# The sums of squares behind the norms: four fp32 matmuls with a column of ones, or four transposes and one VectorE sum over PSUM

## The chip, the cores and the metric

The kernel runs on one core of a Trainium2 chip. The time is device microseconds (us) of one execution. Three runs of the kernel before took 1218.58, 1219.01 and 1220.04 us.

## The reference, cut to what matters

A bidirectional encoder trunk of two layers over a sequence of 512 positions with 1024 features, all in float32. Each layer has two norms over all 1024 features (`g_mix` ahead of the attention part, `g_mlp` ahead of the MLP), two over 256 features (`g_q`, `g_kv`) and one per differential head over 128 features (`g_sub`, four heads); a last norm follows layer two.

```python
def _rmsnorm(x, g, eps=EPS):
    y = x * lax.rsqrt(jnp.mean(x * x, axis=-1, keepdims=True) + eps)
    return y * g

h = x
for l in range(DEPTH):
    z = _rmsnorm(h, g_mix[l]) @ w_in[l]
    c_q, c_kv = _rmsnorm(z[:, 0:256], g_q[l]), _rmsnorm(z[:, 256:512], g_kv[l])
    # eight latent heads from c_q, c_kv; four differential heads from z:
    o = _diff_attention(dq, dk, dv, lam, slopes)        # two softmax maps a head, their difference on dv
    o = _rmsnorm(o, g_sub[l], SUBLN_EPS) * (1.0 - lam_init)
    h = h + concatenate([o_mla, o], axis=-1) @ w_out[l]
    h = h + square(relu(_rmsnorm(h, g_mlp[l]) @ w_up[l])) @ w_down[l]
return _rmsnorm(h, g_final)
```

## The kernel before

Activations lie transposed: features on the 128 partitions, the 512 positions along a row. Every large product is three matmuls on two-part operands (a high and a low part), made by `three` (L1494). Each engine has one program in one fixed order, written out by hand, and engines wait for one another on counting semaphores. Weight blocks come by DMA into two staging buffers; ScalarE makes the high part (L738), VectorE or GpSimd the low part (L1050, L631).

A norm's statistic is needed once per position, summed over features, which is over partitions. It is made in these steps, always in one PSUM bank, `MISC_BANK` (bank 5):

1. ScalarE squares and VectorE adds up the squares of all feature tiles into `ss` (128 x 512); for a differential head, ScalarE leaves the squares of the one tile in `tmp_s[:, 1, :]` (L811).
2. TensorE, `stat_c` (L1504): for each of four groups of 128 positions, one fp32 matmul with the squares as the stationary operand and a column of ones as the moving one. It leaves positions on partitions, in columns 0 to 3 of the bank. It raises `misc_done`.
3. VectorE, `stat_col` (L1062): waits for `misc_done`, writes `rc` = sum/count + eps (128 x 4, L1065), raises `misc_free`.
4. GpSimd, `power` (L608): waits for that, writes `rs` = rc to the power -0.5 (L611), raises `pow_done`.
5. TensorE, `stat_b` (L1513): waits for `pow_done`, then four transposes (L1519) of the broadcast `rs` put the scale of each position on all partitions. VectorE reads it: `stat_row` (L1068) copies it to `rb` or `rb_c`; for a differential head L1354 multiplies with it.

`stat_c` and `stat_col` run 15 times: once for `mix_c` (only in the second layer; the first layer's statistic of the input is made in another way), and in both layers for `q_c`, `kv_c`, four times `sub{g}_c`, and `mlp_c`. The last norm does not use them.

What stands around them. In the part of the latent norms TensorE runs `stat_c` for `q_c` behind the first of four blocks of the `dv` product and `stat_b` for it behind the second (L1742 to L1746); `kv_c` likewise behind the third and fourth. VectorE reaches `stat_col` of `q_c` behind the steps of the rotary key (`krf`, L1254 to L1263) and two `split`s (L1050). For `mlp_c` TensorE runs `stat_c`, half of an up projection's sum (12 matmuls), then `stat_b`. In attention, a loop over steps n: VectorE's order in a step is the inverse softmax sum (L1087), two fused score reads (L1080), then `stat_col` of a head (at n = 8, 12, 16, 20, ahead of L1092), the combination of the two maps (L1092) and the low part of the transposed map (L1112). The first sixteen steps are the differential heads', the next 32 the latent heads' (row maxima L1099, inverse sums L1106).

Of the kernel before, what the change touches and what calls it, by code (L numbers as in the profile page):

```python
# [6 lines left out]
F32 = mybir.dt.float32  # L7
F32R = mybir.dt.float32r
ALU = mybir.AluOpType
ACT = mybir.ActivationFunctionType  # L10
AX_X = mybir.AxisListType.X

P = 128
SEQ, D_MODEL, DEPTH = 512, 1024, 2
KD = D_MODEL // P
TT = SEQ // P
# [197 lines left out]
def trunk(nc, x, w_in, g_mix, g_q, g_kv, w_uq, w_ukv, lam_q1, lam_k1, lam_q2, lam_k2,  # L214
# [3 lines left out]
    def place(name, shape, dt, at=None):  # L218
        size = 4 * int(math.prod(shape[1:]))
        if at is None:  # L220
            at = at_byte[0]
            at_byte[0] += -(-size // 32) * 32
        return nc.alloc_sbuf_tensor_at(name, shape, dt, offset=at)
# [37 lines left out]
    ss = place("ss", [P, SEQ], F32, scratch)  # L261
# [18 lines left out]
    ident = place("ident", [P, P], F32)  # L280
    ones = place("ones", [P, P], F32)
    mhalf = place("mhalf", [P, TT], F32)
    rc = place("rc", [P, TT], F32)
    rs = place("rs", [P, TT], F32)
    rs_mix = place("rs_mix", [P, TT], F32)
    g_rows = place("g_rows", [P, P], F32, region + 16 * kb)
    g_cols = place("g_cols", [P, G_ROWS], F32)
# [14 lines left out]
    with ExitStack() as ctx:  # L302
        bank = [ctx.enter_context(nc.psum_tensor(f"bank{b}", [P, SEQ], F32)) for b in range(8)]
        MISC_BANK, SC_BANKS, TR_BANKS, DV_BANKS = bank[5], bank[2:5], bank[6:8], [bank[2], bank[3], bank[6], bank[7]]
# [5 lines left out]
        def counter(name, per):  # L310

            sem = ctx.enter_context(nc.semaphore(name))
            per_layer[id(sem)] = per
            counters.append(sem)
            return sem

        def once(name):
            return ctx.enter_context(nc.semaphore(name))
# [8 lines left out]
        misc_done, misc_free = counter("misc_done", len(MISC)), counter("misc_free", len(MISC))  # L327
# [30 lines left out]
        u2_added = counter("u2_added", 3)  # L358
        h_turned, h_rows, rows_done, rows_added = (once(n) for n in ("h_turned", "h_rows", "rows_done", "rows_added"))
        sq_summed, mean_made, rs_made, g_out_in = (once(n) for n in ("sq_summed", "mean_made", "rs_made", "g_out_in"))  # L360
        left_made, x_squared, x_left = once("left_made"), once("x_squared"), once("x_left")
        chain_done = counter("chain_done", CHAIN)

# [7 lines left out]
        def val(sem, l, k):  # L371

            return (l + 1) * per_layer[id(sem)] + k
# [87 lines left out]
        def u_low(k):  # L461
            return u_lo[:, (k + KD // 2) % KD, :]
# [566 lines left out]

        @block.vector  # L1030
        def _(dve):
            chain = [0]

            def link(l, ins):

# [18 lines left out]
            def add_square(l, n, first):  # L1054
# [3 lines left out]
                else:  # L1058
                    dve.wait_ge(ss_acc, val(ss_acc, l, n))
                    nc.vector.tensor_tensor(ss[:, :], ss[:, :], tmp_s[:, n % 2, :], ALU.add).then_inc(ss_acc, 1)  # L1060

            def stat_col(l, m, count, eps):  # L1062

                dve.wait_ge(misc_done, val(misc_done, l, m + 1))
                nc.vector.tensor_scalar(rc[:, :], MISC_BANK[:, 0:TT], 1.0 / count, eps, ALU.mult, ALU.add  # L1065
                                        ).then_inc(misc_free, 1)

            def stat_row(l, m, dst):  # L1068
# [162 lines left out]
            for l in layers(dve):  # L1231
                chain[0] = 0

                if l:
                    stat_col(l, MISC_AT["mix_c"], D_MODEL, EPS)
                else:
                    split(0, RING + 1)
# [29 lines left out]
                for b in range(TT):  # L1267
                    split(l, BLOCK_AT[("dv", b)] + RING)
                    if b == 0:
                        stat_col(l, MISC_AT["q_c"], LORA, EPS)  # L1270

                        add_square(l, KD + 2, True)
                        add_square(l, KD + 3, False)
                    if b == 1:
                        stat_row(l, MISC_AT["q_b"], rb_c[:, :])
                        for t in range(KC):
                            nc.vector.scalar_tensor_tensor(out=e_t[:, t, :], in0=e_t[:, t, :],
                                                           scalar=cols(g_cols, G_Q + t, l, KC), in1=rb_c[:, :],
                                                           op0=ALU.mult, op1=ALU.mult).then_inc(c_ready, 1)
                    if b == 2:  # L1280
                        stat_col(l, MISC_AT["kv_c"], LORA, EPS)
                        for t in range(KC):
                            dve.wait_ge(c_hi_made, val(c_hi_made, l, t + 1))
                            nc.vector.tensor_tensor(c_lo[:, t, :], e_t[:, t, :], c_hi[:, t, :].bitcast(F32), ALU.subtract
                                                    ).then_inc(c_lo_made, 1)
# [27 lines left out]
                for n in range(STEPS + 5):  # L1313
# [15 lines left out]
                    g, r = divmod(n - 8, TT)  # L1329
# [159 lines left out]
        def _(pe):  # L1489
            def three(acc, terms, first, last):  # L1490

                for t, ((a_hi, a_lo), (b_hi, b_lo)) in enumerate(terms):
                    for m, (a, b) in enumerate(((a_hi, b_hi), (a_hi, b_lo), (a_lo, b_hi))):
                        mm = nc.tensor.matmul(acc, a, b, start=first and t == 0 and m == 0,  # L1494
                                              stop=last and t == len(terms) - 1 and m == 2)
                return mm

            def wtile(s, k, w=P):
                return w_hi[:, s, k * w:(k + 1) * w], w_lo[:, s, k * w:(k + 1) * w]

            def u(k):
                return u_hi[:, k, :], u_low(k)

            def stat_c(l, m, src=None):  # L1504

                pe.wait_ge(misc_free, val(misc_free, l, m))
                for tt in range(TT):
                    mm = nc.tensor.matmul(MISC_BANK[:, tt:tt + 1], (ss[:, tt * P:(tt + 1) * P] if src is None  # L1508
                                                                   else src[:, tt * P:(tt + 1) * P]),
                                          ones[:, 0:1], start=True, stop=True)  # L1510
                mm.then_inc(misc_done, 1)

            def stat_b(l, m, k):  # L1513
# [173 lines left out]
            for k in range(KD):  # L1687
                pe.wait_ge(u_lo_made, val(u_lo_made, 0, k + 1))
                mm = nc.tensor.matmul(bank[BANK["cq0"]][:, :], wtile(SLOT[0], k)[0], u_low(k), start=False, stop=k == KD - 1)
# [9 lines left out]
            for l in layers(pe):  # L1699


                if l:
                    for use in ("cq0", "cq1"):
                        pe.wait_ge(w_hi_made, val(w_hi_made, l, BLOCK_AT[(use, 0)] + 1))
                        pe.wait_ge(*low_ready(l, BLOCK_AT[(use, 0)]))
                        pe.wait_ge(*taken(l, use))
                    for t in range(KD):
                        pe.wait_ge(u_lo_made, val(u_lo_made, l, t + 1))
                        for use in ("cq0", "cq1"):
                            mm = three(bank[BANK[use]][:, :], [(wtile(SLOT[BLOCK_AT[(use, 0)]], t), u(t))], t == 0, t == KD - 1)  # L1710
                            if t == KD - 1:
                                mm.then_inc(proj_done, 1)
                    pe.wait_ge(ss_acc, val(ss_acc, l, KD))
                    stat_c(l, MISC_AT["mix_c"])
                    head_sum(l, "ckv0", range(KD))
                    stat_b(l, MISC_AT["mix_b"], 0)
                    head_sum(l, "ckv1", range(KD))
# [4 lines left out]
                for t in range(KD):  # L1722
                    for m in range(2):
                        mm = nc.tensor.matmul(bank[BANK["kr"]][:, :], w_hi[:, SLOT[BLOCK_AT[("kr", 0)]], t * P:(t + 1) * P],  # L1724
                                              u(t)[m], start=(t == 0 and m == 0), stop=(t == KD - 1 and m == 1))
# [5 lines left out]
                for b in range(TT):  # L1731
# [3 lines left out]
                    for tt in range(TT):  # L1735
                        for k in range(2):
                            kk = 2 * b + k
                            mm = three(DV_BANKS[tt][:, :], [((u(kk)[0][:, tt * P:(tt + 1) * P],
                                                              u(kk)[1][:, tt * P:(tt + 1) * P]),
                                                             wtile(s, k, SEQ))], kk == 0, kk == KD - 1)  # L1740
# [23 lines left out]
                for n in range(STEPS + 1):  # L1764
                    if DSTEPS < n + 2 < STEPS:
                        scores(l, n + 2)
                    g, r = divmod(n - TT - 2, TT)
# [217 lines left out]
```

## Time and profile before

| | |
|---|---|
| median of three runs | 1219.01 us |
| the profiled execution, its own time | 1218.42 us |
| its span in the trace | 1216.1 us |
| TensorE (PE) busy | 1191.5 us, 98% |
| VectorE (DVE) busy | 892.4 us, 73% |
| ScalarE (ACT) busy | 601.8 us, 49% |
| GpSimd (POOL) busy | 541.8 us, 45% |
| share of the chain that ended last | PE 92%, DVE 4%, ACT 2% |

An engine is called busy while an instruction of its own is in flight; matmuls overlap, so a busy TensorE need not be at its peak. The chain that ended last is followed back from the last instruction, at each step to what released it. In the rows further down a time is us from the span's start; "PEld" is the load of a stationary operand. Two instructions of one engine overlap a little in such rows: the next starts about 0.08 us before the one ahead of it is written as ended, unless it waits.

### The profile page before, as it was taken

The numbers are of one execution on the slowest core, as the hardware profiler recorded it, in microseconds if no ns is written. First come the engines' busy times: TensorE is split into PE (matmuls) and PEld (weight loads), VectorE is DVE, ScalarE is ACT, GpSimd is POOL, SyncE is SP. The second block draws the span as 40 slices with busy tenths as digits, with TensorE's granted clock in tenths as the row PEclk, the third lists the DMA queues.
The fourth block names the chain that finished last, engine by engine and source line by source line (L and its number), as shares of the span: only waits on it lengthen the run. The fifth ranks groups of instructions, "written<-read, shape, count | busy, mean of one in ns | idle before, by whom it ended". The sixth has DMA issues, their size and how long they took to land.

```text
span 1216.1 us, 16360 instructions
## 1 busy us (share of the span) xinstructions
PE 1191.5 (98%) x5700; PEld 975.7 (80%) x5700; DVE 892.4 (73%) x1341; ACT 601.8 (49%) x986; POOL 541.8 (45%) x339
## 2 busy tenths in 40 slices
PE   8999889999999999999999999999999999999997
PEld 7877578888888888888888766788888888888886
DVE  4658967756778776879846688677658678767896
ACT  6345666744544344435423466676444444344443
POOL 1001344622865576556510023446047664766462
PEclk9999999999999999999999998999999999999999
DMA  6521101124234322430324211102252234223402
GB/s 192 138 55 61 45 18 35 53 87 153 75 86 137 115 87 85 130 111 30 104 66 112 61 37 43 36 18 85 73 172 87 78 113 139 86 72 120 139 7 98
DMA packets 128131, 104.55 MB, mean 86 GB/s; under 512 B 5514, under 2 KB 107956, under 8 KB 128052
## 3 DMA queue, kind: packets, MB, share of 16 engines
q1 hardware_dynamic: 127840, 103.50, 28.4%
q8 instruction: 47, 0.77, 0.3%
q14 instruction: 32, 0.26, 0.1%
q10 hardware_dynamic: 84, 0.02, 0.0%
q0 software_dynamic: 128, 0.00, 0.0%
HBM read 99.84 MB, written 2.10 MB: 84 GB/s over the span
## 4 chain that ended last, share of the span: by engine, by line
PE 92%; DVE 4%; ACT 2%; issue 1%; DMA 1%; POOL 0%; SPq 0%; POOLq 0%; DVEq 0%; ACTq 0%
PE bank L1494 82%; PE bank L1561 3%; PE bank L1589 3%; PE bank L1533 2%; DVE pt_lo L1112 1%; PE bank L1508 1%; PE bank L1724 1%; DVE e_t L1092 1%; DMA xin<-in_x 1%; ACT pt_hi L770 0%; DVE k_pack L1158 0%; PE bank L1519 0%; PE bank L1669 0%; DVE v_pack L1151 0%; DVE e_t L1080 0%
## 5 line engine op out<-in xcount | busy, mean ns | idle before, releaser
L1494 PE MATMUL bank<-u_hi,w_hi 128*128 128x512 f32 x760 | 299.4, 394 | 0.3
L1494 PE MATMUL bank<-u_hi,w_lo 128*128 128x512 f32 x760 | 296.1, 390 | 0.0
L1494 PE MATMUL bank<-u_lo,w_hi 128*128 128x512 f32 x760 | 295.8, 389 | 0.0
L738 ACT ACTIVATE w_hi<-stage 128x1024 fp32r<-128x1024 f32 (+3 forms) x141 | 136.4, 976 | 221.0 <-DMA stage<-in_w_up 91.3
L1050 DVE TENSOR_TENSOR w_lo<-stage,w_hi 128x1024 fp32r<-128x1024 f32 (+2 forms) x116 | 134.8, 1171 | 59.8 <-ACT w_hi L738 59.3
L1494 PEld LDWEIGHTS bank<-u_hi,w_hi 128*128 128x128 f32 x760 | 142.7, 188 | 30.8 <-issue 2.5
L1494 PEld LDWEIGHTS bank<-u_hi,w_lo 128*128 128x128 f32 x760 | 142.6, 188 | 30.2
L1494 PEld LDWEIGHTS bank<-u_lo,w_hi 128*128 128x128 f32 x760 | 142.8, 188 | 28.6
L738 ACT ACTIVATE w_hi<-b 128x1024 fp32r<-128x1024 f32 x84 | 88.9, 1059 | 131.8 <-PE bank L1494 105.2
L1494 PE MATMUL bank<-w_hi,quad_hi 128*128 128x512 f32 x392 | 152.6, 389 | 0.0
L1494 PE MATMUL bank<-w_hi,quad_lo 128*128 128x512 f32 x392 | 152.5, 389 | 0.0
L1494 PE MATMUL bank<-w_lo,quad_hi 128*128 128x512 f32 x392 | 152.5, 389 | 0.0
L1050 DVE TENSOR_TENSOR w_lo<-b,w_hi 128x1024 fp32r<-128x1024 f32 x84 | 121.6, 1448 | 24.3 <-ACT w_hi L738 24.3
L1439 DVE TENSOR_TENSOR acc<-acc,bank 128x512 f32<-128x512 f32 x216 | 136.5, 674 | 0.0
L1112 DVE TENSOR_TENSOR pt_lo<-bank,pt_hi 128x512 fp32r<-128x512 f32 x96 | 65.9, 686 | 44.8 <-ACT pt_hi L770 44.2
L1453 DVE SCALAR_TENSOR_TENSOR tmp_y<-bank,rb 128x512 f32<-128x512 f32 x64 | 43.7, 688 | 69.4 <-PE bank L1494 68.7
L611 POOL TENSOR_TENSOR rs<-rc,mhalf 128x4 f32<-128x4 f32 x14 | 18.8, 1340 | 154.4 <-DVE rc L1065 154.4
L1494 PEld LDWEIGHTS bank<-w_lo,quad_hi 128*128 128x128 f32 x392 | 73.6, 188 | 15.3
L1494 PEld LDWEIGHTS bank<-w_hi,quad_lo 128*128 128x128 f32 x392 | 73.6, 188 | 15.2
L1494 PEld LDWEIGHTS bank<-w_hi,quad_hi 128*128 128x128 f32 x392 | 73.6, 188 | 15.2
L636 POOL TENSOR_TENSOR b<-b,b 128x1024 f32<-128x1024 f32 x28 | 81.4, 2909 | 1.1
L624 POOL TENSOR_SCALAR e_t<-e_t,coefs 128x512 f32<-128x512 f32 x64 | 44.3, 694 | 80.5 <-DVE coefs L1106 79.7
(233 smaller groups left out, 2263.4 us busy)
## 6 DMA issues: line engine op xcount, KB each, us to landing
stage<-in_w_up SPq DMA_DIRECT2D x64, 512.0 KB, 4.0
b<-in_w_down SPq DMA_DIRECT2D x56, 512.0 KB, 3.4
stage<-in_w_in SPq DMA_DIRECT2D x32, 512.0 KB, 3.9
stage<-in_w_out SPq DMA_DIRECT2D x16, 512.0 KB, 3.6
stage<-in_w_down SPq DMA_DIRECT2D x8, 512.0 KB, 3.4
xin<-in_x SPq DMA_DIRECT2D x4, 512.0 KB, 6.7
stage<-in_w_ukv SPq DMA_DIRECT2D x4, 512.0 KB, 3.3
out<-yout SPq DMA_DIRECT2D x8, 256.0 KB, 2.3
```

The source lines that it names most:

```text
L611: nc.gpsimd.tensor_tensor(dst[:, :], rc[:, :], mhalf[:, :], ALU.pow).then_inc(pow_done, 1)
L624: nc.gpsimd.tensor_scalar(e_t[:, t, :], e_t[:, t, :], coefs[:, t:t + 1], 1.0, ALU.mult, ALU.mult).then_inc(p_ready, 1)
L636: nc.gpsimd.tensor_tensor(dst[:, :], a[:, :], b[:, :], ALU.subtract).then_inc(t_made, 1)
L738: last = nc.scalar.activation(hi(w_hi, s)[:, :, d:d + n], st(r)[:, :, f:f + n], ACT.Copy)
L1050: last = nc.vector.tensor_tensor(dst, st(r)[:, :, f:f + n], hi(w_hi, s)[:, :, d:d + n].bitcast(F32), ALU.subtract)
L1112: nc.vector.tensor_tensor(piece(pt_lo), TR_BANKS[n % 2].rearrange("p (k c) -> p k c", k=TT), piece(pt_hi).bitcast(F32), ALU.subtract).then ...
L1439: last = nc.vector.tensor_tensor(dst, dst, src, ALU.add)
L1453: nc.vector.scalar_tensor_tensor(out=tmp_y[:, i % 2, :], in0=bank[BANK[use]][:, :], scalar=0.0, in1=rb[:, :], op0=ALU.max, op1=ALU.mult).t ...
L1494: mm = nc.tensor.matmul(acc, a, b, start=first and t == 0 and m == 0, stop=last and t == len(terms) - 1 and m == 2)
L1533: mm = nc.tensor.matmul(SC_BANKS[(2 * n + m) % 3][:, :], a[rows, hd, q], b[rows, :], start=p == 0, stop=p == 2)
L1561: mm = nc.tensor.transpose(TR_BANKS[n % 2][:, kt * P:(kt + 1) * P], e_slot(t)[:, kt * P:(kt + 1) * P], ident[:, :])
L1589: mm = nc.tensor.matmul(MISC_BANK[:, q], v_pack[:, kt, hd, :, :].rearrange("p a c -> p (a c)"), pt[:, kt, q], start=(kt == 0 and pt is pt_ ...
```

## The change

`stat_c` transposes the four 128 x 128 groups of squares into the bank, 512 columns in all, in place of the four matmuls with the column of ones. On VectorE a new `row_sums` waits for `misc_done`, sums the bank over its last 128 columns in each of four groups (one `tensor_reduce`, 128 x 4 from 128 x 512, into the new tile `rsums`) and waits for its own semaphore; `stat_col` then works on `rsums` in SBUF. `misc_free` is still raised by the instruction that writes `rc`. Nothing else is altered: no order of work, no buffer but the new 16 bytes a partition.

```diff
+    rsums = place("rsums", [P, TT], F32)
+        cols_summed = once("cols_summed")
-            chain = [0]
+            chain, summed = [0], [0]
+            def row_sums(l, m):
+
+                dve.wait_ge(misc_done, val(misc_done, l, m + 1))
+                summed[0] += 1
+                nc.vector.tensor_reduce(rsums[:, :], MISC_BANK.rearrange("p (t c) -> p t c", t=TT), AX_X, ALU.add
+                                        ).then_inc(cols_summed, 1)
+                dve.wait_ge(cols_summed, summed[0])
+
             def stat_col(l, m, count, eps):
 
-                dve.wait_ge(misc_done, val(misc_done, l, m + 1))
-                nc.vector.tensor_scalar(rc[:, :], MISC_BANK[:, 0:TT], 1.0 / count, eps, ALU.mult, ALU.add
+                row_sums(l, m)
+                nc.vector.tensor_scalar(rc[:, :], rsums[:, :], 1.0 / count, eps, ALU.mult, ALU.add
                                         ).then_inc(misc_free, 1)
                 # stat_c:
                 pe.wait_ge(misc_free, val(misc_free, l, m))
                 for tt in range(TT):
-                    mm = nc.tensor.matmul(MISC_BANK[:, tt:tt + 1], (ss[:, tt * P:(tt + 1) * P] if src is None
-                                                                   else src[:, tt * P:(tt + 1) * P]),
-                                          ones[:, 0:1], start=True, stop=True)
+                    r = slice(tt * P, (tt + 1) * P)
+                    mm = nc.tensor.transpose(MISC_BANK[:, r], ss[:, r] if src is None else src[:, r], ident[:, :])
                 mm.then_inc(misc_done, 1)
```

## Rows read from the trace of the kernel before

**Rows 1.** The page: busy time of each engine, share of the span, instructions.

```profile
PE 1191.5 (98%) x5700; PEld 975.7 (80%) x5700; DVE 892.4 (73%) x1341; ACT 601.8 (49%) x986; POOL 541.8 (45%) x339
```

**Rows 2.** Windows by engine: stretch, busy us (instructions), granted clock, DMA share, GB/s.

```profile
140.00:160.00 20.00, 15.63 (x83) 11.23 (x82) 17.00 (x38) 12.58 (x29) 6.11 (x7) 1.00 0.07 14
...
740.00:760.00 20.00, 18.48 (x84) 13.67 (x85) 17.25 (x37) 12.29 (x28) 6.08 (x8) 0.84 0.07 14
```

**Rows 3.** The chain that ended last, 115 to 182 us: start, us, what.

```profile
121.62 0.80 PE bank L1508 x8
...
122.44 0.04 DVE rc L1065
```

**Rows 4.** Timeline of PE, first layer: start, us, engine, line, operation, xcount.

```profile
42.87 0.95 PE L1508 MATMUL bank<-ones,ss 128*128 128x1 f32 x8
43.67 0.49 PE L1494 MATMUL bank<-w_hi,u_hi 128*128 128x512 f32 x1
...
49.26 0.60 PE L1519 MATMUL bank<-ident,rs 128*128 128x128 f32 x4
49.61 0.48 PE L1494 MATMUL bank<-w_hi,u_hi 128*128 128x512 f32 x1
...
61.56 0.60 PE L1519 MATMUL bank<-ident,rs 128*128 128x128 f32 x4
```

**Rows 5.** Timeline of DVE outside attention; in brackets the idle time before.

```profile
42.07 0.68 DVE L1256 TENSOR_TENSOR krf<-bank,krf 64x512 f32<-64x512 f32 x1 [3.12 <-ACT krf L882]
42.79 0.68 DVE L1259 TENSOR_TENSOR krf<-krf,ck 64x512 f32<-64x512 f32 x1
...
47.66 0.15 DVE L1065 TENSOR_SCALAR rc<-bank 128x4 f32<-128x4 f32 x1
...
292.78 0.16 DVE L1065 TENSOR_SCALAR rc<-bank 128x4 f32<-128x4 f32 x1 [6.17 <-PE bank L1508]
```

**Rows 6.** Timeline of POOL: the powers of q_c, kv_c, mlp_c, and q_c in layer two.

```profile
47.90 1.13 POOL L611 TENSOR_TENSOR rs<-rc,mhalf 128x4 f32<-128x4 f32 x1 [23.73 <-DVE rc L1065]
57.89 1.39 POOL L611 TENSOR_TENSOR rs<-rc,mhalf 128x4 f32<-128x4 f32 x1 [8.86 <-DVE rc L1065]
...
293.02 1.93 POOL L611 TENSOR_TENSOR rs<-rc,mhalf 128x4 f32<-128x4 f32 x1 [38.22 <-DVE rc L1065]
...
647.20 1.12 POOL L611 TENSOR_TENSOR rs<-rc,mhalf 128x4 f32<-128x4 f32 x1 [24.28 <-DVE rc L1065]
```

**Rows 7.** Timeline of PEld: stationary loads of stat_b for q_c, mlp_c, q_c again.

```profile
49.08 0.53 PEld L1519 LDWEIGHTS bank<-ident,rs 128*128 128x128 f32 x4
...
295.25 0.58 PEld L1519 LDWEIGHTS bank<-ident,rs 128*128 128x128 f32 x4
...
648.43 0.58 PEld L1519 LDWEIGHTS bank<-ident,rs 128*128 128x128 f32 x4
```

**Rows 8.** Timeline of DVE in the first layer's attention, 117 to 181 us.

```profile
121.68 0.68 DVE L1080 CUSTOM_DVE_ANT_0 e_x<-bank,consts 128x512 f32<-128x512 f32 x1
...
122.44 0.16 DVE L1065 TENSOR_SCALAR rc<-bank 128x4 f32<-128x4 f32 x1
...
139.25 0.16 DVE L1065 TENSOR_SCALAR rc<-bank 128x4 f32<-128x4 f32 x1 [0.28 <-PE bank L1508]
...
141.17 0.69 DVE L1342 TENSOR_TENSOR k_pack<-krf,k_pack 64x512 fp32r<-64x512 f32 x1 [0.49 <-ACT k_pack L922]
...
158.34 0.68 DVE L1099 TENSOR_REDUCE nmx<-bank 128x1 f32<-128x512 f32 x1
158.94 0.15 DVE L1065 TENSOR_SCALAR rc<-bank 128x4 f32<-128x4 f32 x1
...
159.86 0.16 DVE L1106 RECIPROCAL coefs<-rsum 128x1 f32<-128x1 f32 x1 [0.18 <-ACT e_t L759]
...
173.15 0.16 DVE L1065 TENSOR_SCALAR rc<-bank 128x4 f32<-128x4 f32 x1 [1.66 <-PE bank L1508]
...
175.37 0.69 DVE L1112 TENSOR_TENSOR pt_lo<-bank,pt_hi 128x512 fp32r<-128x512 f32 x1 [0.21 <-ACT pt_hi L770]
```

## The prediction

> **What bounds the kernel now.** I read the page first, for the busy shares: TensorE is busy 98% of the span, VectorE 73% [rows 1]. So in most places only a shorter or a later TensorE moves the end. Next the windows, for the places where that does not hold: in the differential heads' stretch TensorE is busy 15.63 us of 20 while VectorE has 17.00 [rows 2]. The reader is to see two regimes there: TensorE dense outside, VectorE nearly dense and TensorE with holes inside, from about 121 to 178 us and again in layer two. The chain of waits agrees: it runs on TensorE up to the first head's `stat_c` (121.62, 0.80 us) and goes over to VectorE's `rc` [rows 3]. Last, the timelines of each engine around the 15 statistics, for what is late next.
>
> Seven of the 15 (`mix_c` once, `q_c`, `kv_c`, `mlp_c` twice each) lie where TensorE is dense; eight (`sub0_c` to `sub3_c`, twice) where VectorE's order sets the pace.
>
> **Part 1, TensorE's own time.** From the first record of `stat_c` to the matmul behind it takes 43.67 - 42.87 = 0.80 us. Four transposes of 128x128 fp32 are already in the trace, those of `stat_b`: 49.61 - 49.26 = 0.35 us [rows 4]. So each replacement saves 0.45 us of TensorE where TensorE is dense. The last record ends 0.95 us behind the first before and 0.60 behind with transposes, so VectorE can be released 0.35 us earlier. The bounds of the saving are 0.80 - 0.60 = 0.20 (if the new transposes don't overlap what follows) and 0.45. I take 0.45, since the four in the row run between the same matmuls.
>
> **Part 2, the sum on VectorE.** The trace has a TENSOR_REDUCE of 128x512 from PSUM, of 0.68 us, with 0.60 us to the next instruction when nothing waits (158.34 to 158.94) [rows 8]. It writes one value per partition and not four; that costs at most a few cycles, I add nothing. But the new sum is waited for by the instruction behind it. The same thing is in the trace once, a 0.68 us instruction that the next one waits for: 42.07 to 42.79, 0.72 us [rows 5]. So one sum delays VectorE by 0.60 to 0.72 us; I take 0.72. The instruction for `rc` stays what it is.
>
> A rule of the Trainium skill speaks to this. The row shows 0.72 us with the wait against 0.60 without [rows 5, 8]. "VectorE: DVE Perf Modes", section "The DRAIN you can't avoid", has it that a semaphore between chained VectorE instructions costs nothing extra; by it the sum would be 0.60 us. The same page's "Rules for kernel authors" calls `tensor_reduce` the slowest VectorE operation and advises against it on a hot path, which is a rule against this change.
>
> **Part 3, where TensorE is dense.** Here the question is whether the power on GpSimd still comes before `stat_b`, for TensorE stops there if not.
>
> `q_c`, first layer. VectorE comes to `stat_col` late: it has been busy from 42.07 on and writes `rc` at 47.66, long after TensorE's sum was done at 43.82, so the earlier release is worth nothing. The power runs 47.90 to 49.03 [rows 6], and TensorE loads the first operand of `stat_b` at 49.08 [rows 7]: the power is only just in time. With the sum in front the power ends at 49.75, and the load comes at about 49.80. TensorE is there 0.45 us earlier than before, at 48.63, and stands still for 1.17 us. Net +0.72 us. Behind it on TensorE stands the third `dv` block and everything else. Second layer: power ends at 648.32, load at 648.43, slack 0.11; measured from a time line that `mix_c` has moved up, net 0.72 - 0.06 = +0.66 (0.05 is the gap between a power's end and the load in layer one).
>
> `kv_c`. The power ends at 59.28 and `stat_b` starts at 61.56 [rows 4, 6]; slack 2.28 against 0.72 + 0.45. The saving is kept: -0.45 each. `mix_c` has 24 matmuls between `stat_c` and `stat_b` as `q_c` has, but VectorE there waits for TensorE, as at `mlp_c`; -0.45.
>
> `mlp_c`. VectorE waits 6.17 us for TensorE and starts at once [rows 5], so it gains the 0.35 us. The power starts at 293.02 + 0.72 - 0.35 = 293.39 and ends at 295.32; the load goes from 295.25 to 295.37. Net +0.1 instead of -0.45. I take the second layer alike.
>
> Sum: 0.72 + 0.66 - 3 x 0.45 + 2 x 0.1 = +0.25 us (bounds: -3.15 if the powers are in time by a margin that the GpSimd rows don't show, which are rough; +1.0 if the saving is only 0.20).
>
> **Part 4, the differential heads.** What the idle times behind each `rc` absorb, first layer [rows 8]:
> - `sub0_c` (122.44): VectorE is free at 122.36, so 0.08 us of the earlier release can be used. Net 0.72 - 0.07 = +0.65, on the chain [rows 3]. Behind it wait L1092 and L1112, for them TensorE's transposes, for these ScalarE. Bounds 0.37 and 0.72.
> - `sub1_c` (139.25): VectorE idled 0.28 before, and idles 0.49 before L1342 behind it. 0.72 - 0.28 = 0.44 is less than 0.49: 0.
> - `sub2_c` (158.94): no idle time before; 0.18 before 159.86, of which about 0.27 can be filled with the overlap of two instructions. Net +0.45, bounds 0.3 and 0.72.
> - `sub3_c` (173.15): 1.66 idle before, so the full 0.35 is gained, then 0.21 before 175.37 and about 0.06 of overlap. Net +0.1.
>
> That is 1.2 us a layer, 2.4 us in both, with bounds 1.2 and 3.4. TensorE's 0.45 us is worth nothing here except as the release used above.
>
> **The sum.** +0.25 + 2.4 = +2.65 us on the profiled execution: 1218.42 + 2.65 = 1221.1. That execution lies 0.59 us under the median of the runs shown, so against those 1219.01 + 2.65 = 1221.7 us, +0.22%. What a measurement of this kernel can tell from no change is about 0.2%, 2.4 us.
>
> **The rivals.**
>
> *Hidden on VectorE, TensorE's saving remains (faster).* The place is `stat_b` of `q_c` and `mlp_c` and the differential stretch. If in that stretch idle time further on absorbs the sums, and the power is in time at the four places of part 3, all seven savings count: 7 x 0.45 = 3.15 us, 1215.9 us. It decides from a slack of 1.17 us between power and load. For it: VectorE is idle 27% of the span. Against it: the slacks read are 0.05, 0.11 and 0.30 us, and `rc` of the first head is on the chain.
>
> *A wait on one's own semaphore costs nothing.* Each sum is then 0.60 us. Eight of the 15 pay in full (`q_c`, `mlp_c`, `sub0_c`, `sub2_c`, twice each): 8 x 0.12 = 0.96 us less, 1220.7 us, within 0.2%. For it: nothing in these rows; against it, 42.07 to 42.79. The page named in part 2 would have it so.
>
> *The longer stretch costs TensorE's clock.* In layer two the granted clock fell to 0.84 over 740 to 760 us, in layer one it stayed at 1.00 with TensorE less busy [rows 2]. A mean of 0.84 is 1.2 in place of 2.4 GHz for 0.32 of the 20 us, 6.4 us, in which 3.2 us of full-speed work is not done; the same stretch of layer one has holes of 4.37 us. So one fall costs between 0 and 3.2 us; I take 1.25, nearer to hidden. One more fall per layer gives 1221.7 + 2.5 = 1224.2 us. What speaks for it is the fall that is there; against it, that the longer holes grow by 1.2 us in 40 only.
>
> *Only half arrives in the differential stretch.* ScalarE's and GpSimd's order there are chains of their own; if they are late already, `sub2_c` and half of `sub0_c` go under: 2.4 - 1.5 = 0.9, and 1220.2 us.
>
> **How the numbers follow.** The forecast 0.45, whose own range is 1220.7 to 1223.0. The free wait 0.1, half arriving 0.22, clock 0.13, hidden 0.1. Slower by over 0.2% is above 1221.45: 0.4 of the forecast and of its near neighbours on the upper side, with the clock, makes 0.53. Faster is nearly all of the hidden case: 0.08. Within: 0.39. Range 1218.3 to 1224.2: it leaves out most of the hidden case and the ends of the clock's.
>
> **What would show each step.** Between `stat_c`'s first record and the next matmul 0.35 us in dense places (part 1). A TENSOR_REDUCE of 0.68 us and 0.72 us to `rc` (part 2). TensorE standing about 1.2 us before `stat_b` of `q_c`, with GpSimd's L611 as releaser, and 0.5 us before that of `mlp_c` (part 3). The stretch from `sub0_c` to the dense part longer by 1.2 us in each layer (part 4). The forecast is wrong if those stops are missing, if the heads' stretch keeps its length, or if the clock falls elsewhere than before.

## The result: 0.24% slower, and the profile after

The kernel with the change takes 1222.86 us (median of 14 runs, 1219.64 to 1224.93); the kernel before, run beside it, 1219.46 us (14 runs, 1218.32 to 1221.80). The ratio is 1.0024, with a 95% interval from 1.0015 to 1.0032: slower by 1.8 to 3.9 us, with 2.9 us in the middle (the two medians by themselves are 3.4 us apart). 1221.7 us had been forecast, 2.65 us above before. Two executions of kernels further down, one of 2401 us (TensorE's half alone) and one of 3099 us (the norms alone), count as slow and are left out of their medians and ratios.

The page of the changed kernel, busy time (us) by engine and then the chain that ended last by engine:

```profile
PE 1186.2 (97%) x5640; PEld 969.0 (79%) x5640; DVE 902.8 (74%) x1356; ACT 602.4 (49%) x986; POOL 540.9 (44%) x339
...
PE 84%; issue 7%; DVE 5%; ACT 1%; DMA 1%; POOL 1%; SPq 0%; POOLq 0%; ACTq 0%; DVEq 0%
```

TensorE has 60 matmul records fewer (15 statistics, 8 records each before, 4 now) and is busy 5.3 us less; VectorE has 15 instructions more and is busy 10.4 us more [rows 1]. 15 x 0.45 = 6.75 us and 15 x 0.69 = 10.3 us are what the parts would give. Neither sum is the change of the time: it depends on where they lie.

The statistics themselves. Timeline of PE after, first layer (start, us, engine, line, operation; in brackets the idle time before and who ended it):

```profile
57.83 0.60 PE L1519 MATMUL bank<-ident,ss 128*128 128x128 f32 x4
58.19 0.48 PE L1504 MATMUL bank<-w_hi,u_hi 128*128 128x512 f32 x1
...
123.69 0.60 PE L1519 MATMUL bank<-ident,tmp_s 128*128 128x128 f32 x4
...
181.06 0.94 PE L1504 MATMUL bank<-k_pack,q_pack 128*128 128x512 f32 x3 [0.77 <-DVE k_pack L1168]
```

From `stat_c` (of `kv_c` here) to the matmul behind it takes 58.19 - 57.83 = 0.36 us, where it took 0.80 at `q_c` before [rows 4]. Timeline of DVE after, the sum of `q_c` and that of `sub0_c`:

```profile
44.15 0.68 DVE L1266 TENSOR_TENSOR krf<-bank,krf 64x512 f32<-64x512 f32 x1 [2.58 <-ACT krf L884]
...
49.74 0.68 DVE L1068 TENSOR_REDUCE rsums<-bank 128x4 f32<-128x512 f32 x1
50.46 0.17 DVE L1075 TENSOR_SCALAR rc<-rsums 128x4 f32<-128x4 f32 x1
...
124.53 0.69 DVE L1068 TENSOR_REDUCE rsums<-bank 128x4 f32<-128x512 f32 x1
125.25 0.17 DVE L1075 TENSOR_SCALAR rc<-rsums 128x4 f32<-128x4 f32 x1
125.33 0.75 DVE L1102 SCALAR_TENSOR_TENSOR e_t<-e_t,coefs 128x512 f32<-128x512 f32 x1
```

The sum stands 0.72 us ahead of `rc` at both places, and at `sub0_c` what is behind it (L1102) starts 0.80 us after the sum. Where the chain that ended last ran on TensorE and then over one `rc` [rows 3], it now crosses all four sums of the first layer's heads:

```profile
124.61 0.61 DVE rsums L1068
...
141.81 0.61 DVE rsums L1068
...
161.84 0.61 DVE rsums L1068
...
176.17 0.70 DVE rsums L1068
```

That a sum lies on this chain doesn't say that it costs its 0.7 us: the one at 141.81 (`sub1_c`) took the place of idle time, and its stage kept its length (below).

Windows of the granted clock, after (columns as in rows 2), and one of the kernel before behind it:

```profile
5.00:10.00 5.00, 2.93 (x18) 2.46 (x17) 2.81 (x4) 2.63 (x4) 0.00 (x0) 0.83 1.11 345
10.00:15.00 5.00, 5.00 (x18) 4.00 (x17) 2.21 (x4) 3.22 (x6) 1.04 (x1) 0.50 0.87 222
...
140.00:160.00 20.00, 16.09 (x90) 11.17 (x88) 17.07 (x40) 14.47 (x32) 5.86 (x7) 1.00 0.07 15
740.00:760.00 20.00, 17.15 (x89) 12.02 (x86) 17.00 (x39) 14.39 (x32) 5.82 (x7) 0.91 0.07 14
```

```profile
10.00:15.00 5.00, 5.00 (x31) 4.28 (x30) 3.91 (x8) 3.65 (x7) 1.04 (x1) 1.00 0.87 220
```

This is a trap in the pair. From 10 to 15 us TensorE was granted 0.50 in the execution after (1.2 GHz all through) and 1.00 before (2.4 GHz), although nothing that runs there was altered. By the first `stat_b` the two time lines are 31.03 - 27.71 = 3.32 us apart, before the first changed instruction:

```profile
31.03 0.60 PE L1528 MATMUL bank<-ident,rs_mix 128*128 128x128 f32 x4
```

```profile
27.71 0.60 PE L1519 MATMUL bank<-ident,rs_mix 128*128 128x128 f32 x4
```

About 0.3 us of that is the second piece of the input, whose transposes start at 8.54 in place of 8.23 us; the rest goes with the clock. The spans differ by 1219.8 - 1216.1 = 3.7 us, so nearly all of this pair's difference is the start's. Read from it: the lengths of stages, from one named instruction to another. Not from it: the total; that comes from the runs. In us, from `stat_c` to `stat_c` unless said otherwise:

| stage | before | after | forecast | found |
|---|---|---|---|---|
| `q_c` to its `stat_b`, layer 1 | 6.39 | 5.92 | +0.72 | -0.47 |
| its `stat_b` to `kv_c` | 5.91 | 5.90 | 0 | 0 |
| `kv_c` to `sub0_c` | 66.28 | 65.86 | -0.45 | -0.42 |
| `sub0_c` to the first `k_pack` product | 56.17 | 57.37 | +1.2 | +1.20 |
| from there to `mlp_c` | 114.18 | 114.19 | 0 | 0 |
| `mlp_c` to `mix_c` | 328.88 | 328.87 | +0.1 | 0 |
| `mix_c` to `q_c`, layer 2 | 21.58 | 21.27 | -0.45 | -0.31 |
| `q_c` to its `stat_b` | 6.39 | 6.77 | +0.66 | +0.38 |
| its `stat_b` to `sub0_c` | 71.90 | 71.46 | -0.45 | -0.44 |
| `sub0_c` to the first `k_pack` product | 56.73 | 57.47 | +1.2 | +0.74 |
| from there to `mlp_c` | 114.19 | 114.17 | 0 | 0 |
| `mlp_c` to the end of the span | 324.63 | 324.54 | +0.1 | -0.1 |

The last column sums to +0.6 us; the 0.74 is against a stretch that the kernel before ran at 0.84 of the clock between 740 and 760 us [rows 2]. Against 56.17, its length at full clock, layer two's heads pay 1.30 and the sum is about +1.1 (after, these 20 us ran at 0.91).

The stops of TensorE at `stat_b`, from the weight loads (PEld) after, at `q_c`, `mlp_c` and `q_c` of layer two, with the powers of the last two on POOL behind them:

```profile
51.88 0.41 PEld L1528 LDWEIGHTS bank<-ident,rs 128*128 128x128 f32 x4 [0.21 <-POOL rs L613]
...
298.84 0.41 PEld L1528 LDWEIGHTS bank<-ident,rs 128*128 128x128 f32 x4 [0.66 <-POOL rs L613]
...
652.16 0.41 PEld L1528 LDWEIGHTS bank<-ident,rs 128*128 128x128 f32 x4 [1.11 <-POOL rs L613]
```

```profile
296.86 1.93 POOL L613 TENSOR_TENSOR rs<-rc,mhalf 128x4 f32<-128x4 f32 x1 [38.63 <-DVE rc L1075]
...
651.00 1.11 POOL L613 TENSOR_TENSOR rs<-rc,mhalf 128x4 f32<-128x4 f32 x1 [24.25 <-DVE rc L1075]
```

In layer two the stop before `q_c`'s `stat_b` is the forecast 1.1 us, and `mlp_c`'s is 0.66 where 0.5 was said. In layer one it is 0.21, not 1.17.

### The profile page after: what moved, and what is told of

Its sections match the earlier page's. It is cut to its first block, busy times and chain, and to the rows that moved or that the text cites. A ratio compares the mean times of both kernels' runs of the same rounds, so it can differ in the third digit from the quotient of the medians.

```text
span 1219.8 us, 16255 instructions
## 1 busy us (share of the span) xinstructions
PE 1186.2 (97%) x5640; PEld 969.0 (79%) x5640; DVE 902.8 (74%) x1356; ACT 602.4 (49%) x986; POOL 540.9 (44%) x339
## 4 chain that ended last, share of the span: by engine, by line
PE 84%; issue 7%; DVE 5%; ACT 1%; DMA 1%; POOL 1%; SPq 0%; POOLq 0%; ACTq 0%; DVEq 0%
PE bank L1504 74%; PE bank L1570 3%; PE bank L1598 2%; PE bank L1542 2%; DVE pt_lo L1122 1%; DMA stage<-in_w_in 1%; DMA xin<-in_x 1%; ACT w_hi L740 1%; DVE rsums L1068 0%; PE bank L1678 0%; PE bank L1528 0%; DVE v_pack L1161 0%; POOL rs L613 0%; DVE w_lo L1052 0%; DVE e_t L1102 0%
```

## The experiments

Ratios are to runs of the kernel before on the same chip (medians 1219.34, 1218.99 and 1218.82 us on the three chips used), with 95% intervals; differences in us are the ratio times 1219.

**TensorE's half alone.** The transposes stay, the VectorE sum is left out: `rc` is made from the first four columns of the transposed squares, which are not the sums.

```diff
 def stat_col(l, m, count, eps):
-    row_sums(l, m)
-    nc.vector.tensor_scalar(rc[:, :], rsums[:, :], ...
+    dve.wait_ge(misc_done, val(misc_done, l, m + 1))
+    nc.vector.tensor_scalar(rc[:, :], MISC_BANK[:, 0:TT], ...
```

> The transposes without VectorE's sum: rc is made from four columns of the transposed tile, so the statistic is not the sum (left out: the sum over features). Theory (TensorE gains 0.45 us a statistic where it is dense, nothing but the earlier release elsewhere): seven dense places save 3.15 us less what the power on GpSimd eats at q_c (it is only just in time before, so about 0.45 of each of the two q_c savings is lost): 7 x 0.45 - 2 x 0.4 = -2.3 us against before, -0.2%; the stretch of the differential heads changes by less than 0.2 us. Rival (the transposes are not cheaper in place, because the next matmuls wait for them): 0 us.

1217.1 us, ratio 0.9979 (0.9970 to 0.9987; 11 runs): -2.6 us. A further execution of the same kernel gives the lengths of its stages:

> A second look at the transposes without VectorE's sum (left out: the sum over features), for its profile. Theory: TensorE from stat_c to the next product 0.35 us in place of 0.80; the heads' stretch from sub0_c to the dense part 56.2 us as before, less 0.1; no stop before stat_b of mlp_c.

It took 1216.74 us. The heads' stretch is 177.97 - 121.95 = 56.02 us there, against 56.17 before: TensorE's saving is worth only 0.15 us where VectorE sets the pace, and 7 x 0.45 = 3.15 us at most where TensorE does. Of these, 0.46 us arrive at `q_c` of layer one, 0.42 and 0.48 at `kv_c`, 0.48 and 0.50 at `mlp_c`, but only 0.25 at `q_c` of layer two: even without the sum the power comes late there, and the weight load of `stat_b` stands still for 0.47 us. (`mix_c` to `q_c` is 0.90 us longer in this trace, with a stop of 1.31 us for the low part of a weight block that no other trace here has at that place.)

**VectorE's half alone.** The fp32 matmuls with the ones are back; the sum reads the bank and is waited for, but `rc` is made from the matmuls' columns.

```diff
 # stat_c: matmuls with ones, as before; stat_col:
     row_sums(l, m)
-    nc.vector.tensor_scalar(rc[:, :], rsums[:, :], ...
+    nc.vector.tensor_scalar(rc[:, :], MISC_BANK[:, 0:TT], ...
```

> VectorE's sum and its wait are added, the four matmuls with ones stay, and rc is made from them as before (the sum's result is not used). Theory: q_c +0.7 twice, mlp_c 0.72 less a slack of 0.3, so +0.4 twice, mix_c and kv_c 0; in the heads' stretch sub0_c +0.72, sub1_c +0.2, sub2_c +0.45, sub3_c +0.45 a layer, 1.8 twice: +5.8 us against before, +0.48%. Rival (VectorE's sum is hidden): within 0.5 us of before. Rival (a wait on one's own semaphore is free): 0.60 us from the sum to the next instruction in place of 0.72, and +4.8 us.

1225.27 us, ratio 1.0044 (1.0031 to 1.0057; 5 runs): +5.4 us. With the -2.6 of TensorE's half that makes +2.8, and the whole change measured +2.9. The totals add up, but their intervals are wide (about 1.9 us to each side of the sum), and the stages don't: in the first layer's heads the two halves alone are -0.15 and 58.47 - 56.17 = +2.30 us, the whole change +1.20. So the agreement of the totals is in part chance. Where VectorE sets the pace, the earlier release by the transposes is worth more with the sum there than without; part of the 2.30 may be clock, which was 0.91 to 0.93 in that stretch, though in layer two, at 1.00 up to 760 us, it is still 58.20 - 56.17 = +2.03.

**The heads alone, and the seven norms alone.** `new(m)` picks where the change applies; elsewhere `stat_c` and `stat_col` are those of before.

```diff
+def new(m): return MISC[m].startswith("sub")        # heads alone
+def new(m): return not MISC[m].startswith("sub")    # norms alone
```

> The change at the eight statistics of the differential heads alone, the seven others as before. Theory: +1.2 us in each layer's heads' stretch, +2.4 us against before (+0.2%), 0 elsewhere. Rival (only half arrives there): +0.9 us. Rival (the longer stretch costs clock): more than +3.5 us, with a granted clock below 1.00 in both layers between 120 and 180 us after a layer's start.

1221.18 us, ratio 1.0018 (1.0010 to 1.0027; 11 runs): +2.2 us. It is the cleanest view of part 4, since its clock was 1.00 in both stretches. Timeline of PE of this kernel, first and last instruction of the stretch, layer one and two:

```profile
122.34 0.60 PE L1528 MATMUL bank<-ident,tmp_s 128*128 128x128 f32 x4
...
179.70 0.93 PE L1512 MATMUL bank<-k_pack,q_pack 128*128 128x512 f32 x3 [0.78 <-DVE k_pack L1176]
...
722.63 0.60 PE L1528 MATMUL bank<-ident,tmp_s 128*128 128x128 f32 x4
...
779.99 0.93 PE L1512 MATMUL bank<-k_pack,q_pack 128*128 128x512 f32 x3 [0.78 <-DVE k_pack L1176]
```

179.70 - 122.34 = 57.36 and 779.99 - 722.63 = 57.36 us, against 177.62 - 121.45 = 56.17 before: +1.19 in each layer, 2.4 in both.

> The change at the seven statistics of the wide and latent norms alone (mix_c, q_c, kv_c, mlp_c), the heads' as before. Theory: q_c +0.7 in layer one unless TensorE's clock is low in the first 20 us (then VectorE is less late there and q_c gives -0.35), q_c +0.6 in layer two, three times -0.45, mlp_c about 0 twice: between -1.1 and +0.25 us against before, so within 0.1%. Rival (the powers are in time, all savings count): -3.15 us, -0.26%.

1218.57 us, ratio 0.9990 (0.9981 to 0.9998; 11 runs): -1.2 us. The seven norms where TensorE is dense win; a cost of 0.25 us had been forecast for them. `stat_b` of `q_c` in layer two stands as in the changed kernel:

```profile
650.93 0.65 PE L1540 MATMUL bank<-ident,rs 128*128 128x128 f32 x4 [0.74 <-POOL rs L618]
```

**The sum twice.** `row_sums(l, m)` is called twice in each `stat_col`.

> The changed kernel with VectorE's sum made twice, each waited for. Theory (a sum costs 0.72 us wherever it is paid): 0.72 more at q_c and mlp_c in both layers and at sub0_c, sub2_c, sub3_c, about 0.65 at sub1_c, whose idle time is used up by the first sum; kv_c and mix_c 0: 4 x 0.72 + 2 x (3 x 0.72 + 0.65) = 8.5 us above the changed kernel, some 11 us above the one before, +0.9%. Rival (a wait on one's own semaphore is free): 7.1 us above the changed kernel. Rival (VectorE's sums are hidden): no more than 1 us above the changed kernel.

1231.81 us, ratio 1.0104 (1.0091 to 1.0118; 4 runs): 9 to 9.8 us above the changed kernel, 0.60 to 0.65 us for each of 15 sums, more than the expected 8.5. The stop before `q_c` in layer two grows from 0.69 to 1.47 us on PE:

```profile
657.32 0.65 PE L1529 MATMUL bank<-ident,rs 128*128 128x128 f32 x4 [1.47 <-POOL rs L613]
```

In the heads, `sub0_c` to `sub1_c` is 0.70 us longer than in the changed kernel, `sub1_c` to `sub2_c` 0.63, `sub3_c` to the end 0.72. The first sum was absorbed at `sub1_c` and `sub3_c`; the second finds nothing left. `sub2_c` to `sub3_c` is 1.86 us longer (2.04 in layer two), 1.1 to 1.3 more than the second sum, with a granted clock of 0.91 from 160 to 180 and from 760 to 780 us where the changed kernel had 1.00. By its stages the kernel is 10.7 us longer than the changed one; without these 2.5 us it would be 8.2, near the 8.5.

**The change at `mix_c` and `kv_c` alone.**

```diff
+def new(m): return MISC[m] in ("mix_c", "kv_c")
```

> The change at mix_c and kv_c alone, the three places where the power on GpSimd has over 1 us to spare. Theory: 3 x -0.45 = -1.35 us against before, -0.11%, and no stop of TensorE at stat_b. Rival (the transposes give nothing in place): 0.

1218.22 us, ratio 0.9992 (0.9983 to 1.0001; 11 runs): -1.0 us. The direction is as expected, and the interval just reaches no change.

**`stat_col` of `q_c` earlier.** The changed kernel, and the kernel before, with VectorE's `stat_col` of `q_c` ahead of the `split` of the first `dv` block instead of behind it.

```diff
 for b in range(TT):
+    if b == 0: stat_col(l, MISC_AT["q_c"], LORA, EPS)
     split(l, BLOCK_AT[("dv", b)] + RING)
```

> The changed kernel with VectorE's stat_col of q_c moved ahead of one split (1.15 us earlier). Theory: TensorE's stop before stat_b of q_c, 1.1 us in layer two of the changed kernel's profile, goes; in layer one between 0.2 and 1.2 us, less if TensorE was slow in the first 20 us. So 1.3 to 2.3 us below the changed kernel, +0.05 to +0.15% against before; what is left is the heads' stretch. Rival (the stop is not on the path): no change from the changed kernel, +0.24%. Rival (the split that is now later stops TensorE at its block): also no gain, with a stop in the dv product.

1220.61 us, ratio 1.0011 (1.0002 to 1.0020; 11 runs): +1.3 us, where the changed kernel had +2.9. The stop before `stat_b` in layer two falls from 0.69 to 0.36 us and the stage from 6.77 to 6.45. It was expected to go altogether: `rc` came 1.13 us earlier behind `stat_c` (4.23 against 5.36 us). But the power, which now runs while VectorE makes a `split`, took 1.91 us in place of 1.11; it took 1.91 to 1.93 in every kernel with the move, in both layers. At `mlp_c`, where VectorE also makes a `split` meanwhile, it takes 1.93. What slows it was not tested. POOL, layer two:

```profile
649.34 1.91 POOL L613 TENSOR_TENSOR rs<-rc,mhalf 128x4 f32<-128x4 f32 x1 [23.17 <-DVE rc L1075]
```

The rows give this move 0.32 us, the ratios 1.6; the stretch of the heads in this trace is taken up again further down.

> The kernel before with VectorE's stat_col of q_c ahead of one split and nothing else. Theory (before the change the power was just in time, so TensorE never stopped there): within 0.1% of before, about 0 us. Rival (the move itself is what makes the kernel with the change at five places faster): -0.13%.

1218.98 us, ratio 1.0003 (0.9994 to 1.0013; 11 runs). In the kernel before the move is worth nothing: there the power was in time.

**A version that beats both.** The change at `mix_c`, `kv_c` and `q_c` with the move; then at all seven norms with the move. The heads stay as before.

```diff
+def new(m): return MISC[m] in ("mix_c", "kv_c", "q_c")    # first
+def new(m): return not MISC[m].startswith("sub")          # second
```

> The kernel before with the change at mix_c, kv_c and q_c only, and VectorE's stat_col of q_c ahead of one split. Theory: five savings of 0.45 us, -2.25 us, -0.18% against before. Rival (the stop at q_c stays): -1.35 + 0.6 = -0.7 us.

1217.18 us, ratio 0.9987 (0.9978 to 0.9995; 11 runs): -1.6 us, where -2.25 was expected; the stop at `q_c` of layer two is still 0.36 us.

> The change at all seven wide and latent norms, with stat_col of q_c ahead of one split; the heads' statistics as before. Theory: the same as with the change at five places, since mlp_c gives nothing (its power comes too late for what TensorE saves): -2.0 us, -0.16%. Rival (mlp_c saves 0.45 twice): -3.1 us.

1217.12 us, ratio 0.9990 (0.9981 to 0.9999; 11 runs): -1.2 us. The two cannot be told apart: at `mlp_c` the change gives nothing that shows. Both intervals lie below 1; neither kernel can be told from the one with `mix_c` and `kv_c` alone. The heads' stretch of the first of them, PE, layer two:

```profile
721.99 0.95 PE L1531 MATMUL bank<-ones,tmp_s 128*128 128x1 f32 x8
...
778.16 0.93 PE L1513 MATMUL bank<-k_pack,q_pack 128*128 128x512 f32 x3 [0.77 <-DVE k_pack L1176]
```

It has its old length, 56.17 us.

**The wait on its own semaphore.** VectorE's half alone once more, without `dve.wait_ge(cols_summed, summed[0])`. That is free of races here only because `rc` does not read the sum.

> As the kernel with VectorE's sum alone (matmuls with ones kept, the sum's result not used), but without the wait for the sum. If a wait on one's own semaphore costs 0.12 us, as the rows before the change have it, the time from the sum's start to the next instruction is 0.60 us in place of 0.71, and the whole is about 1 us below the kernel with the wait. If the wait is free, both show the same time between the two starts.

1222.87 us, ratio 1.0035 (1.0021 to 1.0048; 4 runs): about 1 us less than with the wait by the ratios (1.0044), 2.4 by the medians; the intervals overlap. The rows settle it. Timeline of DVE at `sub2_c`, with the wait and then without:

```profile
160.73 0.67 DVE L1068 TENSOR_REDUCE rsums<-bank 128x4 f32<-128x512 f32 x1
161.44 0.16 DVE L1075 TENSOR_SCALAR rc<-bank 128x4 f32<-128x4 f32 x1
```

```profile
160.67 0.68 DVE L1068 TENSOR_REDUCE rsums<-bank 128x4 f32<-128x512 f32 x1
161.27 0.15 DVE L1074 TENSOR_SCALAR rc<-bank 128x4 f32<-128x4 f32 x1
```

0.71 against 0.60 us here; over all 15 places 0.71 to 0.73 with the wait and 0.60 to 0.61 without.

## Why the prediction was right, and the step in it that was not

**Part 1, right.** 0.36 us in place of 0.80. Where TensorE is dense and nothing is late behind it, the saving arrives: -0.47, -0.42, -0.44 in the table. At `mix_c` only 0.31 of it does.

**Part 2, right.** 0.72 us from the sum to `rc`; the sum itself is 0.68 to 0.69 us, four values per partition costing no more than one. The rival of the free wait is refuted by the two pairs of rows above: 0.11 us a wait. "VectorE: DVE Perf Modes", section "The DRAIN you can't avoid", in the Trainium skill has it, from a chain of eight `tensor_copy`, that a semaphore between chained VectorE instructions costs nothing extra; these rows disagree for the instructions here, and the measurement decides. The same page's advice against `tensor_reduce` on a hot path held in the heads and not in the dense part.

**Part 4, right to a tenth of a us.** 1.20 and 1.19 us a layer against 1.2, at the places named: `sub0_c` to `sub1_c` is 0.60 longer, `sub1_c` to `sub2_c` 0.03 shorter, `sub2_c` to `sub3_c` 0.60 longer, `sub3_c` to the end 0.03 longer (forecast 0.65, 0, 0.45, 0.1). The total is closer than its parts: `sub2_c` was put 0.15 us too low. The rival in which half goes under is refuted by the lengths. With the heads alone +2.2 us was measured (1.2 to 3.3) against 2.4.

**Part 3, the mis-sized term.** +0.25 us had been forecast for the seven norms; the change at these alone measured -1.2 us (-2.3 to -0.2), and their stages sum to -1.4 in the pair of traces. The error is mostly `q_c`.

In layer one the forecast took both engines' times from one execution in which the power was 0.05 us ahead of TensorE. But they are not paced by the same thing. VectorE's line to `rc` starts when ScalarE has split a weight block that a DMA brought (42.07, 3.12 us idle [rows 5]), TensorE's by its own products since the start. In the execution after, TensorE reached `stat_c` of `q_c` 3.14 us later than before (46.01 against 42.87), VectorE its `krf` only 2.08 later (44.15 against 42.07). VectorE had gained 1.06 us on TensorE. The slow clock of this start is not needed for that: with the heads alone, at a granted clock of 1.00 from 5 to 20 us, `krf` started 1.94 us ahead of `stat_c`. Over thirteen traces of this series it lay 0.80 to 2.14 us ahead, and the profile before, with 0.80, is the lowest of them. So `rc` began 4.45 us behind `stat_c`, although the sum stood in front of it; before it was 4.79. The 0.72 us was covered, the stop was 0.21, and 0.47 of saving arrived. VectorE's half alone says the same: its `stat_c` came at 43.62, `stat_b` at 50.01, 6.39 us as before, with the sum in front. Timeline of ACT, before and after, the split that waits for the DMA and the `krf` that VectorE waits for:

```profile
40.29 1.06 ACT L738 ACTIVATE w_hi<-stage 128x1024 fp32r<-128x1024 f32 x1 [3.31 <-DMA stage<-in_w_in]
41.38 0.59 ACT L882 ACTIVATE krf<-bank 64x512 f32<-64x512 f32 x1
```

```profile
42.36 1.06 ACT L740 ACTIVATE w_hi<-stage 128x1024 fp32r<-128x1024 f32 x1 [3.20 <-DMA stage<-in_w_in]
43.45 0.60 ACT L884 ACTIVATE krf<-bank 64x512 f32<-64x512 f32 x1
```

Whether a stop of 1.17 us appears in an execution in which VectorE is as late as in the profile before, no trace of the changed kernel shows. The nearest is VectorE's half without the wait: `krf` started 0.96 us ahead of `stat_c` (43.47), and TensorE did stop at `stat_b`, for 0.51 us at the weight load. The transposes would have brought TensorE there 0.45 us earlier still.

```profile
50.11 0.41 PEld L1528 LDWEIGHTS bank<-ident,rs 128*128 128x128 f32 x4 [0.51 <-POOL rs L613]
```

So the wait that the forecast named exists in layer one too; what it had wrong was to take the slack of one execution, 0.05 us, for that of all.

In layer two the stop is there as forecast. The weight load of `stat_b` comes 652.16 - 645.39 = 6.77 us behind `stat_c`, before 648.43 - 642.26 = 6.17 [rows 7]: +0.60 against +0.66. But what counts is the matmul behind the load, and its record moved by 0.38 only. Before, the load ran 0.22 us ahead of its matmul (648.43 and 648.65); after, where TensorE stands still, both records begin at 652.16. The forecast charged the load's delay to the matmul.

`mlp_c` shows the same: the load 298.84 - 295.25 = 3.59 us behind `stat_c`, before 295.25 - 291.80 = 3.45 [rows 7], so +0.14 against the forecast +0.1; the matmul 3.59 against 3.67, -0.08; and over the whole stage nothing. Adding `mlp_c` to the last version moved nothing either.

The move of `stat_col` ahead of one `split` halves the stop of layer two. It is the smaller of two reasons why the last versions win; the larger is that the heads are left alone.

**Why the sum came out all the same.** The stages say about +1.1 us at full clock, the heads alone and the norms alone together 2.2 - 1.2 = +1.0, and the whole was measured at +2.9 (1.8 to 3.9). The first two agree with each other; the intervals of the parts together (about 1.5 us to each side) reach the whole. Part of the rest is clock: over 14 runs the changed kernel's mean granted clock was 0.9955, over 77 runs of the kernel before (those beside the experiments) 0.9965, and a line through these runs gives about 0.4 us for each 0.001, so some 0.4 us. The six runs of the changed kernel at 0.996 took 1222.1 us on average, the seven of the kernel before at 0.996 1219.6: at equal clock 2.5 us are left. That it is the longer heads' stretch that lowers the clock was not shown: the heads alone had 0.9974. About 1.4 us of the 2.9 stays without a place, which the width of the interval (1 us to each side) covers in part.

One trace shows something of this size. The changed kernel with the move has the same heads' stretch, but in layer one its `sub2_c` to `sub3_c` took 18.40 us in place of 16.95. In both kernels TensorE was busy 2.7 of 4 us and then stood still for 2.1 us behind `pt_lo`; in one the granted clock fell after it, in the other it did not. Windows (columns as in rows 2) of the kernel with the move, and of the changed kernel at the same place:

```profile
160.00:164.00 4.00, 2.68 (x10) 2.32 (x11) 2.39 (x6) 2.83 (x7) 1.71 (x2) 0.67 0.00 0
```

```profile
162.00:166.00 4.00, 2.62 (x16) 2.30 (x17) 3.27 (x8) 2.89 (x7) 1.71 (x2) 1.00 0.00 0
```

Such a fall costs 1.45 us, near the 1.25 that the clock's rival took for one. In the kernel before, the fall of layer two cost 16.94 - 16.35 = 0.59 us in the same stretch. How many executions have one, and whether the change makes them more frequent, no experiment here counts. The forecast total was inside the interval partly by luck: `q_c` was made too dear by about 1.5 us, and something of that size was not in the sum.

**The rivals.** All seven savings counting, with the powers in time, would have been -3.15: at `q_c` in layer one it came true, in layer two and at `mlp_c` not, and the heads took back more. One more clock fall per layer, 1224.2 us: not borne out as a rule, for the falls in the traces come and go (740 to 760 us: 0.84 before, 0.91 after, 1.00 with the heads alone), but not refuted either. A fall now and then, at 1.45 us each, is the one thing the rows show that could fill what the stages leave open. "Only half arrives", 1220.2 us, fails by the heads' lengths, as said.

## What to carry to other kernels

An edit that moves work from one engine to another is not good or bad as a whole: it wins where the relieved engine is dense and the loaded one has slack until the next meeting point, and loses where the order is the other way round; apply it place by place, here at three of the five kinds of statistic and with one `stat_col` moved, and a loss of 0.24% (0.15 to 0.32) turns into a gain of 0.13% (0.05 to 0.22). A slack of 0.05 us between two engines that are paced by different things (a DMA here, the engine's own products there) is not a constant of the kernel: before charging a stop, look at what paces each of them. Compare two traces by the lengths of stages between named instructions, never by their spans, and take the total from many runs.

## What the runs showed of the hardware

- The first 20 us differ from one execution to the next with the same instructions in them: from 10 to 15 us the granted clock was 0.50 in some profiles and 1.00 in others, and the first `stat_b` came between 27.61 and 31.09 us. This spread is larger than the whole effect of the change. The clock is not all of it: among those with 1.00 it was 27.61 to 30.21 us.
- A VectorE instruction that waits for the one ahead of it on a semaphore starts 0.70 to 0.73 us after it, one that doesn't 0.60 to 0.61 (the one ahead takes 0.68 us).
- A `tensor_reduce` of 128x512 fp32 from PSUM takes a median of 0.686 us into four values per partition, as into one [rows 8].
- Four fp32 matmuls with one moving column are twice as many records (x8) and take 0.80 us of TensorE, four fp32 transposes of 128x128 (x4) 0.36.
- The power on GpSimd (128x4 fp32) took 1.11 to 1.13 us at `q_c` and, with nothing changed in it, 1.91 to 1.93 when it ran beside a VectorE `split` of 128x1024.
- With the same work around a stop of 2.1 us on TensorE, the granted clock fell in one execution (0.67 over 4 us) and stayed at 1.00 in another; the stretch was 1.45 us longer with the fall.
